# Second half of a block's norm and projection in one program behind an expert stage, with four places for turned keys

## The reference

```
hn = (_rms(x, norm1_g) * (1 + sc1) + sh1)
proj = hn @ w_in
fq, fk, fv, ff, mq, mk, mv, mi, mf, mo, bq, bk, bv = split(proj)
y_fox  = fox_attention(rms(fq), rms(fk), fv, ff + bias)      # 6 heads, decay by the gates ff
h_ml   = mlstm(silu(conv(mq)), silu(conv(mk)), mv, mi, mf)   # 4 heads, gates mi and mf
y_moba = moba_attention(rms(bq), rms(bk), bv, slopes)        # 6 heads, a bias by distance
x = x + g1 * (concat(y_fox, y_ml, y_moba) @ w_out)
x = x + g2 * feed_forward(...)
```

## Time and profile before

| what | value |
|---|---|
| median of 3 runs | 2493.03 us (2487.32 to 2505.91) |
| the profiled execution | 2484.72 us, its span 2482.9 us |
| busy: PE, DVE, ACT, POOL | 2029.9, 1730.1, 606.7, 1037.8 us |
| mean granted TensorE clock | 0.921 of full speed |
| DMA | 676.48 MB, 272 GB/s over the span; the gathers are 536.94 MB of it |
| expert stage of the program above | until 1845.7 us |
| norm of half b | 1846.7 to 1858.4 us |
| projection of half b | 1858.7 to 1960.5 us |
| attention of half b | from 1960.8 us |

### The profile page before, as it was taken

One profiled execution on the slowest core, in us unless ns is written; L12 is line 12 of the kernel. 1 busy time (PEld: TensorE's weight loads), 2 busy tenths in 40 slices (PEclk: granted clock), 3 DMA queues, 4 the chain that ended last, 5 costly groups with the idle time before them and its releaser, 6 DMA issues. The chain is left out here.

```text
span 2482.9 us, 25393 instructions
## 1 busy us (share of the span) xinstructions
PE 2029.9 (82%) x7625; PEld 1293.4 (52%) x7625; DVE 1730.1 (70%) x3557; ACT 606.7 (24%) x1399; POOL 1037.8 (42%) x1086
## 2 busy tenths in 40 slices
PE   4985766988786977787987978876968797999999
PEld 4963544545332443343543434433428674788887
DVE  4865536999987876777766888888757473544464
ACT  2124412343232222112211142322121232110121
POOL 0001013667776776667765767777740000000000
PEclk8996787999998989889999989989998898999999
DMA  4751017999999999999998999999974202233222
GB/s 166 272 212 68 18 51 251 380 389 396 408 402 404 392 403 398 406 406 403 385 402 338 403 409 403 402 404 398 409 271 159 98 1 68 68 101 93 76 86 100
DMA packets 263737, 676.48 MB, mean 272 GB/s; under 512 B 22605, under 2 KB 111042, under 8 KB 263618
## 3 DMA queue, kind: packets, MB, share of 16 engines
q0 software_dynamic: 147456, 536.94, 55.1%
q1 hardware_dynamic: 116162, 138.13, 16.6%
HBM read 672.87 MB, written 2.10 MB: 272 GB/s over the span
## 5 line engine op out<-in xcount | busy, mean ns | idle before, releaser
L2208 PE MATMUL bank<-arena 128*128 128x512 f32 x1536 | 787.8, 645 | 174.8 <-DMA arena<-in_peer_v,arena 148.6
L2439 DVE SCALAR_TENSOR_TENSOR arena<-arena,h_ps 128x1024 f32<-128x1024 f32 x512 | 615.3, 1217 | 182.0 <-DMA arena<-in_peer_u,arena 174.0
L2169 POOL DMA_INDIRECT arena<-in_peer_v,arena x512 | 516.4, 1009 | 234.7 <-issue 129.9
L2169 POOL DMA_INDIRECT arena<-in_peer_u,arena x512 | 504.5, 985 | 220.6 <-issue 135.9
L2208 PEld LDWEIGHTS bank<-arena 128*128 128x128 f32 x1536 | 290.1, 203 | 523.0 <-issue 264.8
L2452 DVE SCALAR_TENSOR_TENSOR x<-arena,x 128x1024 f32<-128x1024 f32 x128 | 164.5, 1285 | 42.4 <-DMA arena<-in_peer_v,arena 30.9
L2293 ACT ACTIVATE arena<-ident,arena 128x128 f32<-128x128 f32 x384 | 135.8, 393 | 58.1 <-PE bank L2208 30.9
L142 DVE CAST parts<-arena 128x2048 fp32r<-128x2048 f32 (+4 forms) x60 | 68.2, 1136 | 113.6 <-DMA arena<-in_w_gate_up 73.1
L1453 PE MATMUL bank<-hT,arena 128*128 128x256 f32 x512 | 123.7, 398 | 21.6 <-DMA arena<-in_peer_w_q 20.2
L144 DVE TENSOR_TENSOR parts<-arena,parts 128x2048 fp32r<-128x2048 f32 (+4 forms) x60 | 126.7, 2111 | 4.5
L1453 PEld LDWEIGHTS bank<-hT,arena 128*128 128x128 f32 x512 | 102.4, 201 | 48.7 <-DMA arena<-in_peer_w_q 21.7
(11 more groups left out here) (422 smaller groups left out, 3301.6 us busy)
## 6 DMA issues: line engine op xcount, KB each, us to landing
arena<-in_w_ada SPq DMA_DIRECT2D x12, 2048.0 KB, 9.6
arena<-in_w_in SPq DMA_DIRECT2D x15, 1536.0 KB, 6.7
arena<-in_w_gate_up SPq DMA_DIRECT2D x44, 512.0 KB, 5.0
arena<-in_peer_w_q SPq DMA_DIRECT2D x16, 1024.0 KB, 15.8
arena<-in_w_down SPq DMA_DIRECT2D x22, 512.0 KB, 3.4
arena<-in_peer_u,arena POOLq DMA_INDIRECT x512, 8.6
arena<-in_peer_v,arena POOLq DMA_INDIRECT x512, 8.4
arena<-in_w_in SPq DMA_DIRECT2D x7, 1024.0 KB, 8.0
```

Source lines behind the costliest of these rows:

```text
L2169: nc.gpsimd.indirect_dma_start(out=ring[:, n % R, :], out_offset=None, in_=a[table][0], in_offset=bass.IndirectOffsetOnAxis(ap=expert[:, s ...
L2208: ins = nc.tensor.matmul(psum[half][:, :], diag[:, m % R, :], v_ring[:, n % R, half * 512:(half + 1) * 512], start=(s % PH == 0 and j == 0 ...
L2439: nc.vector.scalar_tensor_tensor(out=u_ring[:, n % R, :], in0=u_ring[:, n % R, :], scalar=1.0, in1=h_ps[:, :], op0=ALU.mult, op1=ALU.mult, ...
```

## The change

The diff, cut to what the text speaks of. The unchanged helpers that moved are left out.

```diff
+        N5_0 = 29 * PK + 4
+        def n5_act(act, tb):        # Ln, drain, Exp for one tile
+        def n5_mean(dve, tb):       # mean for one tile
+        def n5_scale(dve, tb):      # rows[:, tb, :] = x[:, tb, :] * rstd
...
     def score2 (attention, half b)
                 if p.rows_in_k:
+                    pe.wait_ge(rows_moved[h % len(p.kT)], 16 * (h // len(p.kT) + 1))
                     if h == 0:
-                        pe.wait_ge(row_moved, 16 * SM_H)
                         pe.wait_ge(ones_ready, 1)
...
     expert stage, SP, at its end
+                sync.wait_ge(o2_summed, 2)
+                sync.wait_ge(v_used, pe_count(STEPS * PK - R))
+                for i in range(2):
+                    load_b(sync, i)
     expert stage, ACT
+                        if i * PK + j == N5_0:
+                            act.wait_ge(y_added, 3)
+                            nc.scalar.activation(rows[:, 2, :], x[:, 2, :], ACT.Square, accum_out=stat[:, 0, 2:3]).then_inc(b_squared, 1)
+                        if i * PK + j == N5_0 + 2:
+                            act.wait_ge(b_mean, 5)
+                            n5_act(act, 2)
     expert stage, DVE
+                        if i * PK + j == N5_0 + 1:
+                            dve.wait_ge(b_squared, 9)
+                            n5_mean(dve, 2)
+                        if i * PK + j == N5_0 + 3:
+                            dve.wait_ge(b_rstd, 4)
+                            n5_scale(dve, 2)
...
     load_b, tile 8
-                sync.wait_ge(gates_zeroed, 3)
-                for c0, n, at in ((FF0, FOX_H, 0), (MF0, ML_H, MF), (MI0, ML_H, NG + MF)):
-                    sync.dma_start(w_g[:, :, at:at + n], w_in_2[:, :, c0:c0 + n]).then_inc(w_2_loaded[0], 16)
-                sync.dma_start(w_mq, w_in_2[:, :, MQK0:MQK0 + ML_W]).then_inc(w_2_loaded[0], 16)
+                sync.dma_start(raw_b(i)..., w_in_2[:, :, MQK0:MQK0 + ML_W]).then_inc(w_2_loaded[0], 16)
-        norm_T("n5_", x, [(0, D)], rows, hT_of[1], ..., loads=load_first_b, pool_part=zero_gates,
-               parts=split_h_b, tbs=B_TBS)
+        KT_SLOTS = 4
+        rows_moved = [sem(f"row_moved{i}") for i in range(KT_SLOTS)]
+        kT_b, qT_b = view(20992, KT_SLOTS, T), view(6144 + 2048, 2, GT)
+        def move_row(sync, h):
+            if h < KT_SLOTS:
+                sync.wait_ge(conv_ready, 2)
+                sync.wait_ge(g2_done, 2)
+            else:
+                sync.wait_ge(scored, 3 * UNITS + 2 * (h - KT_SLOTS) + 2)
+            sync.dma_start(kT_b[HD:HD + 1, h % KT_SLOTS, :], gate_of[1].bias[h:h + 1, :]).then_inc(rows_moved[h % KT_SLOTS], 16)
     projection, SP: behind the loads
+                for h in range(KT_SLOTS):
+                    move_row(sync, h)
     projection, POOL: the clearing of gate_of[1].bias and conv_q_of[1], and the iota (moved here)
     projection, PE: first the transposes
+                for k in range(KD):
+                    if k >= 4:
+                        pe.wait_ge(b_copied, 3 * KD + k - 3)
+                    for b in range(2):
+                        if k == 0 and b == 1:
+                            pe.wait_ge(b_normed, 10)
+                        ins = nc.tensor.transpose(psum[4 + k % 4][:, b * P:(b + 1) * P], rows[:, 2 + b, k * P:(k + 1) * P], ident[:, :])
+                    ins.then_inc(b_turned, 1)
     ... and in the first pass over tile 8
+                            if i == 0 and j == 0:
+                                pe.wait_ge(h_split, k + 1)
     projection, ACT: first n5_act for tb 3 and the eight evacuations
-                    if i == 7:
+                    if i == 6:
                         rms_square(act, 1, 1)
-                    if i == 8:
+                    if i == 7:
                         rms_exp(act, 1)
     projection, DVE
+                nc.vector.scalar_tensor_tensor(out=rows[:, 3, :], in0=x[:, 3, :], scalar=1.0, in1=x[:, 3, :], op0=ALU.mult, op1=ALU.mult, accum_out=stat[:, 0, 3:4])
+                dve.drain()
+                n5_mean(dve, 3)
+                split_gates()                     # of w_g_a, 576 elements in a row
+                dve.wait_ge(b_rstd, 5)
+                n5_scale(dve, 3)
+                split_b(0)
+                for k in range(KD):
+                    dve.wait_ge(b_copied, 3 * KD + k + 1)
+                    split_h_b(dve, k).then_inc(h_split, 1)
+                split_b(1)
-                    if i == 7:
-                        rms_reduce(dve, 1, 0)
-                    if i == 8:
-                        rms_reduce(dve, 1, 1)
-                for b in range(2):
-                    rms_scale(dve, 1, b)
+                    if i in (6, 7):
+                        rms_reduce(dve, 1, i - 6)
+                    if i in (8, 9):
+                        rms_scale(dve, 1, i - 8)
     attention, SP
-                for h in range(SM_H):
-                    sync.dma_start(kT_b[HD:HD + 1, h, :], gate_of[1].bias[h:h + 1, :]).then_inc(row_moved, 16)
                 (loads of w_out and the gain)
+                for h in range(KT_SLOTS, SM_H):
+                    move_row(sync, h)
```

More of the change, by code:

```diff
@@ L1493, in program @@
         GATE_BIAS = (("fox_f_bias_2", 0, FOX_H, 0), ("ml_f_bias_2", 0, ML_H, MF), ("ml_i_bias_2", 1, ML_H, MF))
+        N5_0 = 29 * PK + 4
+        def n5_act(act, tb):
+            nc.scalar.activation(stat[:, 0, tb:tb + 1], stat[:, 0, tb:tb + 1], ACT.Ln)
+            act.drain()
+            nc.scalar.activation(rstd[:, 0, tb:tb + 1], stat[:, 0, tb:tb + 1], ACT.Exp, scale=-0.5).then_inc(b_rstd, 1)
+        def n5_mean(dve, tb):
+            nc.vector.tensor_scalar(stat[:, 0, tb:tb + 1], stat[:, 0, tb:tb + 1], 1.0 / D, EPS, ALU.mult, ALU.add).then_inc(b_mean, 1)
+        def n5_scale(dve, tb):
+            nc.vector.tensor_scalar(rows[:, tb, :], x[:, tb, :], rstd[:, 0, tb:tb + 1], None, ALU.mult).then_inc(b_normed, 1)
         class Gates:
@@ L2137, in block2_dve, with width_b, raw_b, parts_b @@
                 o2_add(dve, 0, 1, psum[6:8])
+        ORDER_B = [8, 9, 2, 3, 4, 5, 6, 7, 0, 1]
+        GM = KD * (2 * NG + ML_W)
+        raw_at, part_at = (X2, Y2), (0, 6144)
+        w_high, w_low = ([{n: view_r(at + d, KD * n) for n in (384, ML_W, 2 * NG + ML_W)} for at in part_at] for d in (3072, 0))
+        w_split, loaded_by = sem("w_2_split"), [16 * 5, 16 * 5]
+        def width_b(i):
+            return 2 * NG + ML_W if ORDER_B[i] == 8 else TILES_2[ORDER_B[i]][1]
+        def raw_b(i):
+            return view(raw_at[i % 2], KD * (ML_W if ORDER_B[i] == 8 else width_b(i)))
+        def parts_b(i, at, n):
+            return [of[i % 2][width_b(i)][:, at:at + KD * n].rearrange("p (k n) -> p k n", n=n) for of in (w_high, w_low)]
+        def load_b(sync, i):
+            t = ORDER_B[i]
+            if t == 8:
+                sync.dma_start(raw_b(i).rearrange("p (k n) -> p k n", n=ML_W), w_in_2[:, :, MQK0:MQK0 + ML_W]).then_inc(w_2_loaded[0], 16)
+                return
+            after(sync, w_split, i - 1)
+            c0, n = TILES_2[t]
+            sync.dma_start(raw_b(i).rearrange("p (k n) -> p k n", n=n), w_in_2[:, :, c0:c0 + n]).then_inc(w_2_loaded[i % 2], 16)
+        def count_b(i):
+            return loaded_by[i % 2] + 16 * (i // 2 + 1)
         assert C0 + O2_0 + 2 * KD + 4 <= (STEPS + 1) * PK
@@ L2537, in split_h_b @@
             return split(dve, hT_of[1][:, k, :].rearrange("p (b t) -> p b t", t=P), *h_all_b(k))
[L2539 to L2546, removed]
@@ L2568, in count_b @@
[L2568 to L2581, removed]
@@ L2583, in program @@
-        norm_T("n5_", x, [(0, D)], rows, hT_of[1], gain_cols=lambda k: mod_gain[:, k:k + 1],
-               shift_cols=lambda k: mod[:, SH1 + k:SH1 + k + 1], loads=load_first_b, pool_part=zero_gates,
-               parts=split_h_b, tbs=B_TBS)
-        S0 = len(TILES_2)
-        kT_b, qT_b = view(0, SM_H, T), view(6144 + 2048, 2, GT)
+        S0 = len(TILES_2)
+        h_split = sem("h_split")
+        KT_SLOTS = 4
+        rows_moved = [sem(f"row_moved{i}") for i in range(KT_SLOTS)]
+        kT_b, qT_b = view(20992, KT_SLOTS, T), view(6144 + 2048, 2, GT)
@@ L2626, in _ @@
             def _(act):
+                act.wait_ge(b_mean, 6)
+                n5_act(act, 3)
+                for k in range(KD):
+                    act.wait_ge(b_turned, 3 * KD + k + 1)
+                    nc.scalar.activation(hT_of[1][:, k, :], psum[4 + k % 4][:, 0:GT], ACT.Identity, scale=mod_gain[:, k:k + 1],
+                                         bias=mod[:, SH1 + k:SH1 + k + 1]).then_inc(b_copied, 1)
                 for i, t in enumerate(ORDER_B):
```

34 lines of the change are left out of this document (17 added, 17 removed).

## The result

The changed kernel takes 2473.55 us (median of 11 runs, 2468.15 to 2484.60) against 2489.07 for the kernel before (11 runs, 2483.51 to 2505.91). The ratio is 0.9945 with a 95% interval of 0.9926 to 0.9964: 15.5 us by the medians, 9 to 18 by the interval.

What follows compares the result with a forecast made beforehand. The prediction took the DMA gathers to bound the expert stage, so gains lie only outside it. Terms 9.2 + 1.8 + 6.1 - 0.8 gave 16.3 us, from a median of 2493.03 to 2477 us; range 2466 to 2488.

Steps and rivals of the forecast that it cites:

- Start of half b: From DVE's last add through position 0: first product 9.5 us earlier by a shorter chain, 9.2 us gained in all.
- Earlier norms of queries and keys: Late projection: PE gaps of 1.2 and 1.4 us replace one of 2.6, so position 9 runs faster; 1.8 us gained.
- The attention's first score: Attention's start: PE waits only for the keys, no longer for the row DMAs; 6.1 us gained.
- The loads behind the gathers: End of expert stage: two early weight loads take bandwidth from the last v rows; 0.8 us lost.
- equal shares: Rival at the expert stage's end: early loads take half the last v rows' bandwidth; 3.4 us less gain, 2480, chance 0.13.
- The forecast's own sign: End of expert stage: DVE's last add comes not over 1 us later, counted from the last gather.
- the 3 us that was to prove it wrong: End of expert stage: the prediction is wrong if the last v rows land 3 us or more later.
- The clock in the attention: Attention's first units: no gain counted from a faster clock, as PE still stands still some 4 us at the program boundary.
- The norm of tile 2: Expert stage, step 29: the added ACT and DVE work is hidden by the gathers; costed at nothing.
- New waits in step 29: Rival: ACT and DVE wait for each other, and both new projection gaps cost clock; 2483 us, chance 0.10.
- exposed row moves: Rival in the attention: rows 4 to 11 issued only when due, eight times 2.3 us, 18.6 lost; 2495, chance 0.03.
- The clock staying up: Rival at the attention's start: a shorter PE pause keeps the clock up; up to 3.9 us more gain, 2473, chance 0.17.

Runs made afterwards that it cites:

- before_again: The kernel before, unedited, measured and profiled once more; 2490.11 us, ratio 0.9999.
- rows_only: The kernel before with only the change's four key places, early row moves and one semaphore per place; 2569.90 us on a slower chip, ratio 0.9962.
- again: The changed kernel, unedited, measured and profiled once more; 2476.53 us, ratio 0.9952 to the kernel before.
- rows_late: The changed kernel with the bias rows of heads 0 to 3 moved at the attention's start instead of in the projection; 2472.43 us, ratio 0.9936.
- loads_late: The changed kernel with the first two weight loads issued at the start of the projection's program, not behind the gathers; 2477.67 us, ratio 0.9950.
- load_at_end: The changed kernel with the two early weight loads let go three v rows later; 2561.73 us on a slower chip, ratio 0.9920 to the kernel before.
- sig_gates_wait: The changed kernel with the sigmoid behind the attention, gate sums one position later and early loads three v rows later; 2546.55 us on a slower chip, ratio 0.9862.
- sig_later: The changed kernel with the gate's sigmoid and its table loads moved behind ACT's last work of the attention; 2464.42 us, ratio 0.9905.
- double_load: The changed kernel with two more loads of 512 KB each, which nobody reads, behind the two early weight loads; 2472.30 us, ratio 0.9923.
- norm_late: The changed kernel with the norm of tile 2 moved from step 29 of the gather stage to the projection's start; 2478.86 us, ratio 0.9939.
- keep_busy: The changed kernel with 30 unused products filling 3.5 of PE's 4.3 us pause at the projection's end; 2469.50 us, ratio 0.9910.

## Why the prediction was right, point by point

The time came out 0.8 us from the forecast difference, by the medians. That is closer than the terms deserve, and in part luck: two of them were wrong with the same sign, together by about 4 us, and this hid behind the noise of the runs.

- **Start of half b, forecast 9.2.** Right. The start is 9.64 shorter (forecast 9.5). Its steps: boundary 0.33, squares 1.23, gate split 0.45 and 0.76, scaling 0.74, split 3.5, all within 0.2. Position 0 takes 13.68 us, 0.14 more than in the first profile of before, so the two give 9.5; against before_again and rows_only, where position 0 took 12.78 and 12.56, they give 8.5 to 8.7. The reason for taking 9.2 and not 7.3 failed, though: the clock rose 4.5 us behind the first product in the changed profile, about as late as before. It did not matter: in `again` the clock stood at 1.00 from the first product on and position 0 took 13.68 all the same. This fits the forecast's own picture, in which the splits of DVE pace the first pass.
- **Earlier norms of queries and keys, forecast 1.8.** The profile shows what was worked out: gaps of 1.1 and 1.2 us for one of 2.6, position 9 at 1.00 in 5.7 us instead of 7.4, and positions 1 to 9 shorter by 1.85. It was read from the trace and not undone by a run of its own, so that the new order is the cause is argued, not shown.
- **The attention's first score, forecast 6.1.** Right: 6.06 to 6.81, by whether the clock falls before or behind the turning of the first head. But part of the reasoning was idle. I counted the early issue of the rows as part of the step; rows_late shows that it brings nothing.
- **The loads behind the gathers, forecast -0.8.** This term was mis-sized. The tail is 8.87 to 9.76 us without the early loads (before, before_again, loads_late, rows_only) and 10.93 to 13.77 with them (eight profiles; load_at_end and sig_gates_wait, which hold the loads back, show 8.99 and 8.68). The means are 9.28 and 11.96: 2.7 us, where the bound for equal shares was 4.2. The forecast's own sign, an add not over 1 us later, failed in the changed profile (1.26), and in three of the eight (13.06, 13.45, 13.77 against 9.28) it was over the 3 us that was to prove it wrong. I had taken SP's share from the median landing of a load amid full gathers, 17.2 us; behind the last gathers of the changed kernel the first load landed in 9.8. What the last rows lose is not told by that median: the tail hangs on the one `v` gather that lands last. In sig_later PE waited 4.4 us for a single one.
- **The clock in the attention, forecast 0 with up to 3.9 of gain.** Wrong in sign on the average. The lower level lasted 5 to 28 us behind the first score in the kernels that let it fall, and the attention took 77.8 to 88.5 us, 81.8 in the mean of seven profiles of the change and its variants (changed, again, loads_late, rows_late, double_load, norm_late, load_at_end) against 79.7 for the two of before: some 2 us given back. With only two profiles of before this difference is not shown to be the change's; that the fall costs 2.5 us or more, and that PE's pause of 4.3 us causes it, is. The pause was there before, too.
- **The norm of tile 2, forecast 0 inside the gathers.** Right by norm_late and by the pace of the gathers in steps 29 and 30.
- **The rivals.** New waits in step 29 and exposed row moves did not appear: of the 8 later rows none released a score. Equal shares came true in part. The clock staying up did not happen in the change, and is what sig_later and keep_busy make of it.

Sum of the measured terms: 8.5 to 9.5, + 1.85, + 6.1 to 6.8, - 2.7, - 2.1, which is 11.7 to 13.4 us, inside the 9 to 18 us of the run times. The difference to the median's 15.5 is not larger than what their interval allows.

## What to carry to other kernels

Before moving a transfer ahead, look at which single arrival ends the stage in front of it: by the profiles, three rows of patience turned a move that won nothing net into one that wins some 2.4 us at the start for a tail as short as before. When a wait is removed, ask what let the consumer depend on it; here it was one semaphore for twelve rows, and not the moment of the issue. A pause of PE at a program boundary is paid twice if the clock falls in it; here ACT's table loads, which made that pause, could stand behind the next stage.

## What the runs showed of the hardware

The granted clock, once fallen to the lower level, came back after very different times of unbroken work: PE was busy for 27.8 us in norm_late and 19.3 us in the changed kernel before it rose, 7.9 us before, and in the changed kernel's projection it rose 4.5 us behind the first product. Pauses of 1.0 and 1.2 us left it at 1.00, one of 2.6 in the projection and one of 4.3 ahead of the attention did not, and one of 3.08 among the gathers did, so the length of the pause alone does not decide. Ahead of the attention the clock fell 1.9 us (loads_late) to 5.4 us (rows_late) behind the last product of the projection.

What a fall costs follows from how long it lasts. The level of 0.50 lasted, behind the first score, 5.0 us in loads_late, 5.2 in load_at_end, 7.8 before, 8.2 in double_load, 9.4 in rows_only, 10.5 in before_again, 10.6 in `again`, 19.3 in the changed kernel, 19.5 in rows_late and 27.8 in norm_late. With the four profiles that never fell, all fourteen attentions lie within 0.1 us of 75.3 us plus 0.47 us for each us at the lower level. So the clock explains all of the attention's spread of 10.8 us between these profiles (77.8 to 88.5 where it fell), 4.1 of it between two executions of the same kernel (84.5 and 80.3), which is as much as most of the parts of this change are worth.

The Trainium skill, "TensorE: Matmul & The Clock Gate", section "Part 1: The HAM clock gate (the "warmup" mystery)", leads one to expect the upper level soon after steady work begins. The 4.5 us of the projection are near to that; the 19.3 and 27.8 us of the attention are not, and there the measurement decides.
